# One trunk layer on one core: scale sums straight into columns, x normalised earlier, chunk pairs block by block, norm sums broadcast by one product

## The reference, cut to what matters

```python
cf = silu(c)
mod = cf @ mod_w + mod_b                     # 1024 x 6144
sh1, sc1, g1, sh2, sc2, g2 = split(mod, 6)
h = rmsnorm(x, norm1_g) * (1 + sc1) + sh1
x = x + g1 * mixer(h, w_in, ..., w_up_s5, w_up_mlstm, w_up_fox, w_out)
h = rmsnorm(x, norm2_g) * (1 + sc2) + sh2
x = x + g2 * ((silu(h @ w1) * (h @ w3)) @ w2)
return rmsnorm(x, final_g)
# rmsnorm(x, g) = x * rsqrt(mean(x*x, -1) + 1e-6) * g
```

## Time and profile before

| | us |
|---|---|
| median of 3 runs (lowest, highest) | 883.72 (883.39, 883.77) |
| the profiled execution's own time | 883.69 |
| its span in the profile | 881.9 |
| TensorE busy | 845.0, 96% |
| VectorE busy | 444.0, 50% |
| ScalarE busy | 325.1, 37% |
| GpSimd busy | 32.9, 4% |
| TensorE's granted clock, mean over the span | 0.989 |

### The profile page before, as it was taken

How to read it: one execution, slowest core, us unless ns; L and a number is a source line. 1 busy time by engine, 2 the same in 40 slices (tenths; PEclk the granted TensorE clock), 3 DMA queues, 4 the chain that set the end, 5 groups by cost and what they waited for, 6 DMA issues and landing times.

```text
span 881.9 us, 10466 instructions
## 1 busy us (share of the span) xinstructions
PE 845.0 (96%) x3892; PEld 673.8 (76%) x3892; DVE 444.0 (50%) x720; ACT 325.1 (37%) x477; POOL 32.9 (4%) x46
## 2 busy tenths in 40 slices
PE   3899999999999999999999799999999999999996
PEld 0478888877887777787888578888888888888885
DVE  6689977246778744234873363333333333322222
ACT  4455445443223444333333553333333332222221
POOL 1100000000000000000002110000000000000110
PEclk9999999999999999999999889999999999999999
DMA  8923422257785122114233223333333333333322
GB/s 295 296 74 90 107 73 72 72 157 250 261 286 168 48 62 58 49 48 162 78 96 120 71 57 99 100 100 97 95 95 95 95 95 90 90 107 90 98 75 95
DMA packets 149370, 100.65 MB, mean 114 GB/s; under 512 B 11072, under 2 KB 142552, under 8 KB 148312
## 3 DMA queue, kind: packets, MB, share of 16 engines
q1 hardware_dynamic: 146080, 100.10, 37.2%
q10 hardware_dynamic: 3256, 0.10, 0.2%
HBM read 97.03 MB, written 2.10 MB: 112 GB/s over the span
## 4 chain that ended last, share of the span: by engine, by line
PE 89%; DVE 5%; ACT 3%; issue 1%; DMA 1%; SPq 1%; POOL 0%; DVEq 0%; ACTq 0%
PE bank L1607 25%; PE bank L1609 25%; PE bank L1608 25%; PE bank L1624 2%; PE bank L1801 2%; PE bank L1731 1%; PE bank L1823 1%; PE bank L1751 1%; PE bank L1762 1%; DMA modA<-in_mod_w 1%; PE bank L1848 1%; PE bank L1814 1%; PE bank L1799 1%; DVE wlo L1113 1%; ACT whi L631 1%
## 5 line engine op out<-in xcount | busy, mean ns | idle before, releaser
L1607 PE MATMUL bank<-h_lo,whi 128*128 128x512 f32 x712 | 287.3, 404 | 8.4 <-DVE h_lo L1135 4.3
L1609 PE MATMUL bank<-h_hi,wlo 128*128 128x512 f32 x712 | 279.1, 392 | 0.0
L1608 PE MATMUL bank<-h_hi,whi 128*128 128x512 f32 x712 | 279.0, 392 | 0.0
L1607 PEld LDWEIGHTS bank<-h_lo,whi 128*128 128x128 f32 x712 | 134.7, 189 | 41.8 <-issue 9.7
L1609 PEld LDWEIGHTS bank<-h_hi,wlo 128*128 128x128 f32 x712 | 134.6, 189 | 28.9
L1608 PEld LDWEIGHTS bank<-h_hi,whi 128*128 128x128 f32 x712 | 134.9, 189 | 28.5 <-issue 1.7
L1113 DVE TENSOR_TENSOR wlo<-raw,whi 128x1024 fp32r<-128x1024 f32 x61 | 74.6, 1223 | 105.8 <-ACT whi L631 105.8
L631 ACT ACTIVATE whi<-raw 128x1024 fp32r<-128x1024 f32 x61 | 64.4, 1055 | 156.4 <-PE bank L1609 111.7
L1609 PE MATMUL bank<-a_hi,wlo 128*128 128x512 f32 x176 | 68.5, 389 | 0.0
L1607 PE MATMUL bank<-a_lo,whi 128*128 128x512 f32 x176 | 68.5, 389 | 0.0
L1608 PE MATMUL bank<-a_hi,whi 128*128 128x512 f32 x176 | 68.5, 389 | 0.0
(11 more groups left out here) (319 smaller groups left out, 979.6 us busy)
## 6 DMA issues: line engine op xcount, KB each, us to landing
raw<-in_ffn_w SPq DMA_DIRECT2D x60, 512.0 KB, 3.8
raw<-in_w_in SPq DMA_DIRECT2D x44, 512.0 KB, 4.0
slab<-in_mod_w SPq DMA_DIRECT2D x32, 512.0 KB, 6.0
modA<-in_mod_w SPq DMA_DIRECT2D x4, 1024.0 KB, 11.9
modB<-in_mod_w SPq DMA_DIRECT2D x4, 1024.0 KB, 19.6
raw<-in_w_out SPq DMA_DIRECT2D x8, 512.0 KB, 3.7
raw<-in_ffn_w SPq DMA_DIRECT2D x8, 384.0 KB, 3.2
xtok<-in_x SPq DMA_DIRECT2D x4, 512.0 KB, 5.5
```

The lines of the kernel that those rows point to most:

```text
L1607: mm(dst, w_h, m_l, start=first, stop=False)
L1608: mm(dst, w_h, m_h, start=False, stop=False)
L1609: return mm(dst, w_l, m_h, start=False, stop=last)
```

## The change

- `mod_rows` becomes `mod_scale`: for each block of `mod_w`, eight products with a 128x128 piece of the scale half as the weights and one column of `cf` as the moving side, all accumulated in the columns of PSUM bank 7. `modrow`, its two ACT copies and their products go; the shift sums stay (`mod_shift`). The x transposes come after blocks 0 to 3 instead of 2 to 5.
- VectorE normalises x between the two `exact_exp` calls.
- GpSimd's `vm` and `qpad` memsets wait for all of `h_lo` as well.
- Chunks 0 and 1 of `w_in`, and `w1`'s and `w3`'s first, are multiplied in turn for each block k.
- Before the last `w_out` chunk's residual, ScalarE and VectorE split the two first FFN chunks.
- The norm's sums: ones (128x128) times `sqa` is issued inside the last `w_out` chunk, ones times the last square behind it, both 512 columns wide into bank 6. So each partition has all sums. ScalarE's Sqrt and VectorE's reciprocal then run over 128x512 (`rb`), and `dg`, its product and the four-column steps go. The last norm, at the end of the kernel, keeps its form.

```diff
-            for k in range(KB):
-                mod_rows(k)
-                if 2 <= k < 6:
-                    x_transposes(2 * (k - 2))
-                    x_transposes(2 * (k - 2) + 1)
+            def mod_scale(k):
...
+                pe.wait_ge(s_mod0[k], 16)
+                for i in range(KB):
+                    ins = mm(ps[7][:, KB + i:KB + i + 1],
+                             (modA, modB)[k // 4][:, k % 4, D + i * P:D + (i + 1) * P], cf[:, k:k + 1],
+                             start=(k == 0 and i == 0), stop=(k == KB - 1 and i == KB - 1))
...
+            for k in range(KB):
+                mod_scale(k)
+                if k < 4:
+                    x_transposes(2 * k)
+                    x_transposes(2 * k + 1)
+            mod_shift()
```

```diff
             exact_exp(c_(DT), None, ldt)
+            dve.wait_ge(s_std, 1)
+            link(V.reciprocal(rstd[:], rstd[:]))
+            for t in range(NT):
+                V.tensor_scalar(xtok[:, t], xtok[:, t], rstd[:, t:t + 1], None, ALU.mult).then_inc(s_xn, 1)
             tt(c_(T3), c_(DT), are, ALU.mult)
             exact_exp(c_(MAG), c_(EM1), c_(T3))
```

```diff
# GpSimd
-            pool.wait_ge(s_mod1, 3)
+            pool.wait_ge(s_mod1, 2)
+            pool.wait_ge(s_hlo, KB)
             nc.gpsimd.memset(vm[:, :, :, MD], 1.0).then_inc(s_pad, 1)
             nc.gpsimd.memset(qpad[:], 0.0).then_inc(s_pad, 1)
```

```diff
# TensorE, the first two chunks
-            for s in range(NA):
+            pe.wait_ge(w_lo, 2)
+            for k in range(KB):
+                pe.wait_ge(s_hlo, k + 1)
+                for s in range(2):
+                    ins = split_mm(ps[s][:], whi[:, s, k], wlo[:, s, k], h_hi[:, k], h_lo[:, k], k == 0, k == KB - 1)
+                    if k == KB - 1:
+                        ins.then_inc(w_mm, 1)
+            for s in range(2, NA):
```

```diff
# TensorE, last w_out chunk and the FFN's start
+                    if n == KB - 1 and k == KB - 2:
+                        pe.wait_ge(s_x2c, KB)
+                        pe.wait_ge(s_sqa, KB - 2)
+                        mm(ps[6][:], ones[:], sqa[:], start=True, stop=False)
...
-            sum_squares(sqa, sq[:, (KB - 1) % 2], 0)
-            pe.wait_ge(s_dg, 1)
-            mm(ps[2][:], ones[:], dg[:].rearrange("p t n -> p (t n)"), start=True, stop=True).then_inc(s_rb, 1)
+            mm(ps[6][:], ones[:], sq[:, (KB - 1) % 2], start=False, stop=True).then_inc(s_ssb, 1)
+            pe.wait_ge(w_lo, S_F1 + 2)
+            for k in range(KB):
...
+                for w in range(2):
+                    s = S_F1 + w
+                    ins = split_mm(ps[w][:], whi4[:, s % 4, k], wlo[:, s % 4, k], h_hi[:, k], h_lo[:, k],
+                                   k == 0, k == KB - 1)
```

```diff
# ScalarE and VectorE at the same place
-            act.wait_ge(s_sqmm, 1)
-            A(rstd[:], ps[6][:, 0:NT], ACT.Sqrt, bias=epst[:, 0:1], scale=1.0 / D).then_inc(s_std, 1)
+            act.wait_ge(s_ssb, 1)
+            A(rb[:], ps[6][:], ACT.Sqrt, bias=epst[:, 0:1], scale=1.0 / D).then_inc(s_rb, 1)
...
             for n in range(S_F1 - 3 - S_OUT, KB):
+                if n == KB - 1:
+                    lo4(S_F1)
+                    lo4(S_F1 + 1)
...
+            V.reciprocal(rb[:], rb[:]).then_inc(s_rr, 1)
...
-                V.tensor_tensor(htmp[:, k % 4], x1g[:, k], ps[2][:], ALU.mult).then_inc(s_h2, 1)
+                V.tensor_tensor(htmp[:, k % 4], x1g[:, k], rb[:], ALU.mult).then_inc(s_h2, 1)
```

More of the change, by code:

```diff
@@ L850, in _ @@
             for n in range(S_F1 - 3 - S_OUT, KB):
+                if n == KB - 1:
+                    act.wait_ge(w_mm, S_F1 - 1)
+                    for s in range(S_F1, S_F1 + 2):
+                        act.wait_ge(w_loaded[s % 4], SLOT_LOADS[s])
+                        A(whi4[:, s % 4], raw[:, s % 4], ACT.Copy).then_inc(w_hi, 1)
                 act.wait_ge(s_col, n + 1)
@@ L1024, in _ @@
             tt(c_(M4), c_(M4), c_(M4), ALU.mult)
[L1025 to L1028, removed]
             fq0 = V_BIN + VB["fq"]
@@ L1510, in _, with lo4 @@
                     residual(n, n % 2, 16)
+            def lo4(s):
+                dve.wait_ge(w_hi, s + 1)
+                V.tensor_tensor(wlo[:, s % 4], raw[:, s % 4], whi4[:, s % 4].bitcast(F32),
+                                ALU.subtract).then_inc(w_lo, 1)
             for n in range(S_F1 - 3 - S_OUT, KB):
+                if n == KB - 1:
+                    lo4(S_F1)
+                    lo4(S_F1 + 1)
                 dve.wait_ge(w_mm, S_OUT + n + 1)
@@ L1520, in h2_lo @@
                                        ).then_inc(s_hlo, 1)
[L1522 to L1531, removed]
             dve.wait_ge(s_rb, 1)
+            V.reciprocal(rb[:], rb[:]).then_inc(s_rr, 1)
+            dve.wait_ge(s_rr, 1)
             for k in range(KB):
@@ L1616, in _ @@
             tr(ps[5][:, 0:P], rows1[:], ident[:]).then_inc(t_rows, 1)
-            def mod_rows(k):
+            def mod_scale(k):
                 pe.wait_ge(s_cf, 1)
-                pe.wait_ge(t_cols, 2)
                 pe.wait_ge(s_mod0[k], 16)
[L1623 to L1628, removed]
+                for i in range(KB):
[3 more added lines that the diff above has]
+                if k == KB - 1:
+                    ins.then_inc(s_mod1, 1)
             def x_transposes(k):
@@ L1636, in x_transposes, with mod_shift @@
                 ins.then_inc(s_xt, 1)
[L1638 to L1642, removed]
+            def mod_shift():
+                pe.wait_ge(s_modd, 1)
+                for i in range(KB):
+                    ins = mm(ps[7][:, i:i + 1], modA[:, 0, i * P:(i + 1) * P], ones[:, 0:1], start=True, stop=True)
                 ins.then_inc(s_mod1, 1)
@@ L1955, in _ @@
                     x_again(n - 1)
[L1957 to L1963, removed]
             for n in range(KB):
@@ new lines, in _ @@
+            for k in range(KB):
+                if k in H2_POOL:
+                    pe.wait_ge(s_hlop, H2_POOL.index(k) + 1)
+                else:
+                    pe.wait_ge(s_hlo, KB + k + 1 - sum(j < k for j in H2_POOL))
+                for w in range(2):
+                    s = S_F1 + w
+                    ins = split_mm(ps[w][:], whi4[:, s % 4, k], wlo[:, s % 4, k], h_hi[:, k], h_lo[:, k],
+                                   k == 0, k == KB - 1)
+                    if k == KB - 1:
+                        ins.then_inc(w_mm, 1)
@@ L1986, in _ @@
+            for w in range(2):
+                s = S_F1 + 2 + w
+                pe.wait_ge(w_lo, s + 1)
+                for k in range(KB):
+                    ins = split_mm(ps[2 + w][:], whi4[:, s % 4, k], wlo[:, s % 4, k], h_hi[:, k], h_lo[:, k],
+                                   k == 0, k == KB - 1)
+                ins.then_inc(w_mm, 1)
+            with pe.Fori(0, NF // 2 - 1) as i:
                 for u in range(2):
                     for w in range(2):
-                        s = S_F1 + 2 * u + w
+                        s = S_F1 + 4 + 2 * u + w
@@ L1989, in _ @@
                         pe.wait_ge(w_lo, i * 4 + (s + 1))
                         if w == 0:
-                            pe.wait_ge(s_act, i * 2 + (1 + u))
-                            if u == 1:
-                                pe.wait_ge(s_h2, KB)
+                            pe.wait_ge(s_act, i * 2 + (3 + u))
                         for k in range(KB):
[L1995 to L1999, removed]
@@ L2024, in _ @@
                     pe.wait_ge(s_sq, 2 * KB)
-                    sum_squares(sqa2, sq2[:, (KB - 1) % 2], 8)
+                    for t_ in range(NT):
+                        cols = slice(t_ * P, (t_ + 1) * P)
+                        mm(ps[6][:, 8 + t_:9 + t_], sqa2[:, cols], ones[:, 0:1], start=True, stop=False)
+                        ins = mm(ps[6][:, 8 + t_:9 + t_], sq2[:, (KB - 1) % 2, cols], ones[:, 0:1],
+                                 start=False, stop=True)
+                    ins.then_inc(s_sqmm, 1)
                     pe.wait_ge(s_col, 2 * KB)
```

47 lines of the change are left out of this document (13 added, 34 removed).

## The result

| | before | after |
|---|---|---|
| median of 4 runs (lowest, highest), us | 883.75 (883.39, 884.74) | 898.25 (894.97, 901.48) |
| the profiled execution's own time, its span, us | 883.69, 881.9 | 894.97, 893.2 |
| scale sums begin, `modc` | 15.66, 39.97 | 15.32, 52.60 |
| fourth `w_in` chunk begins | 64.02 | 76.90 |
| last residual, first `htmp` | 496.99, 503.86 | 510.77, 517.51 |

The changed kernel is slower. The ratio is 1.0149, 95% interval 1.0118 to 1.0181; the medians are 14.5 us apart, the two profiled executions 11.3.

What follows compares the result with a forecast made beforehand. TensorE, busy 96% of the span, was taken as the bound, with time to be had only where it waits or runs slow. Terms +14.6 - 1.0 + 1.25 + 0 - 1.1 = +13.8 on 883.72 gave 897.5 us, range 889 to 901.

Steps and rivals of the forecast that it cites:

- rivals 1, 2 and 3: Alternatives to the forecast total; the third: slow loads as forecast but a cheap reciprocal at the FFN, 894.6 us, 5%.
- Part 1: Start, up to modc: scale sums straight into columns, many weight loads at the slow clock, +14.6 us.
- The term of the loads: Scale sums at the start: 128 issues, each behind its load, at 0.212 us each, 27.1 us.
- rival 2: Scale sums: loads take 0.116 us at either clock, or one-column products raise it; total 881.8 us, 10%.
- Rival 1: Scale sums: bursts of x transposes raise the clock, making four of eight blocks quick; total 891 us, 12%.
- Part 2: Start: x normalised between the exponentials; shift sums end later, about 36.2 us, but TensorE is far behind: 0.
- Part 3: After modc: later memset frees hs, -1.0 us, but holds a tensor_scalar ahead of lo(3), +1.25 us.
- Part 4: First w_in chunks paired by block: chunk 2 stalls 1.3 us for evacuation, but lo(3) sets the fourth chunk: 0.
- Part 5: FFN's start: broadcast norm with a dear reciprocal, +0.6 us; paired chunks split early, -1.7 us; together -1.1 us.

Runs made afterwards that it cites:

- wide_first: Changed kernel plus six useless 512-column products before the first block of scale sums; 901.99 us, one execution.
- wide_between: Two kernels: changed kernel plus six useless 512-column products before the first block and one or two after each block; 911.89 and 899.18 us.
- rows_back: Changed kernel with the wide scale rows, row copies and their column products restored, all else kept; 884.06 us, ratio 0.9983 to the kernel before.
- best: Kernel before plus chunk pairs, early split of the first FFN chunks, later qpad memset, earlier lo(3), narrow norm sums over sqa issued early; 881.34 us, ratio 0.9957.
- after_again: The changed kernel, unaltered, measured again on another chip; 896.43 us, ratio 1.0134 to the kernel before.
- scale_only: Kernel before with only the scale sums put straight into columns, x transposes after blocks 1 to 4; 899.57 us, ratio 1.0136.
- best_fill: best plus useless 512-column products: two before the first chunk pair, one before and two behind the product with dg; 879.82 us, ratio 0.9940.

## Why the prediction was right, and where its sizes were off

It was right in its sign and its cause: the loss is that of the scale sums at the slow clock, and rivals 1, 2 and 3 fell. That the time fits to 0.75 us, 897.5 forecast and 898.25 measured, is luck: the sum has 13.8, the profiled executions differ by 11.3, and the median lies higher for a reason that isn't in the sum (last paragraph of this section).

**Part 1**, forecast +14.6, was +12.63 (52.60 - 39.97). The term of the loads held: 27.3 for 27.1, and 3.4 for the shift sums. The transposes were mis-sized: the upper bound of 8.2 was taken, and four bursts took 4 x 1.60 = 6.4. The start was 0.34 earlier than taken. That the clock doesn't rise in this stage, the step on which everything hung, is shown by the pace itself, 0.213 to the end of the shift sums, which is that of the rows at a granted clock of 0.50 in wide_first; the wide_between kernels show the price at either clock. So rival 2 is out by its mechanism, not only by its time. The Trainium skill, "TensorE: Matmul & The Clock Gate", LDWEIGHTS, gives a load as columns over 1.2 GHz and doesn't bring in the clock gate, for 128 columns an estimate of 107 ns; here one issue with its load took 115 ns at full clock and 213 at half, so the measurement differs from the page at the slow clock. Rival 1 is out too: after each burst of transposes the next block again took 3.41. (Its four quick blocks come to 6.2 by its own figures, 4 x (3.4 - 1.86), not to 6.5.)

**Part 2**, forecast 0, is 0 in the changed kernel: VectorE waited 4.75 for rstd (5.3 forecast) and the shift sums were done at 36.04 (36.2). rows_back shows what the cover was worth: with a quick TensorE the later shift sums are on the path, for 0.8 us.

**Part 3**, -1.0 and +1.25: `hs` to the last `h_lo` took 9.38 (9.3 forecast, 10.3 before), and the held `tensor_scalar` 1.33. From `modc` to the fourth chunk are 24.30, before 24.05: +0.25, as the sum has it. The trace agrees with the Trainium skill, "SBUF — State Buffer", Who interferes with whom: beside the memset the `tensor_tensor` took its 1.23, the `tensor_scalar` was held to the memset's end.

**Part 4**, forecast 0 with a new stall of 1.3, had the stall at 1.19, and `lo(3)` was later still, by 1.53. Right. In best, where `lo(3)` comes early, the fourth chunk has no wait; the stall for the evacuation, 1.19, is left, and one of 0.34 for the fifth chunk's `lo`.

**Part 5**, forecast -1.1, was 0.90 - 0.13 - 1.95 = -1.2. The reciprocal took 3.35 (3.4), residual to `htmp` 6.74 (6.66 and the 0.85 ahead of it), `htmp` to the pair's end 15.47 (15.7).

**What the sum did not have** goes with medians further apart than the profiled executions, 14.5 against 11.3: falls of the clock between 240 and 400 us, which after_again shows and the first profile has not. The forecast's 897.5 is near the median because an over-sized term happens to be about as large as they are. Such falls are in the profiles of after_again, scale_only, best_fill and the three kernels with wide products, and not in those of the kernel before, the changed kernel's first, rows_back and best; the before executions on two chips spread by 6 to 8 us as well. Whether the change makes them more frequent there, by what it shifts at the start, is open: only one execution of each run has a trace, and none of the experiments sets them apart.

## What to carry to other kernels

A sum over the partitions into columns is one product for each 128 outputs, each behind its own load; before trading wide row products for it, count the loads and price them at the clock that the stage will have once the wide products are gone. A scalar per token is cheaper rooted and inverted on four columns and then laid out by a product than laid out first, since the reciprocal over 512 columns costs more than the product that it saves. Where chunks start on data that comes block by block, working two of them through in turn, with their weights and those of the next chunks split early, was worth 1.95 us at the FFN and 1.4 at the start of best (with the memset moved as well); the changed kernel, whose third chunk waits for the first's evacuation and whose fourth for its weights, gained nothing from it at the start (24.30 against 24.05).

## What the runs showed of the hardware that was not expected

- The granted clock's column reads 1.00 from the start to the first change on record, whatever the clock is: 3.41 us for 16 issues stand beside 1.00 in the changed kernel and beside 0.50 in wide_first. The products' own pace tells the clock.
- TensorE can be busy without a gap and lose the clock or never get it: from 15.3 to 52.6 us here, at 39 us in rows_back, and at 387 us in after_again, each time in or right behind products of 1 to 128 columns.
- The time of one kernel is a spread and not a number: 877.50 to 885.98 for best, 894.97 to 901.48 for the changed kernel, and it falls as the mean clock rises (0.992 at 894.97, 0.985 at 901.48). Between the two traced executions of the changed kernel, falls in the middle of it cover the difference of 5.7 us.
- A reciprocal on VectorE took 3.35 us for 128x512, five times a Sqrt of ScalarE on the same shape (0.69).
